# The HGRN stage of a two-block network: logarithms and scans of the two directions as two items, and the forget weights' split two slots later

## The chip, the cores and the metric

The kernel runs on one core of one Trainium2 chip. The metric is the device time of one execution in microseconds; lower is better. A core has five engines that run their own instruction lists in order and meet through semaphores: TensorE (PE, matmuls), VectorE (DVE), ScalarE (ACT), GpSimd (POOL) and SyncE (SP, which here issues DMAs).

## The reference

`first_block` (a macaron block: feed-forward, token mixing, feed-forward) is followed by `second_block` (sparse attention beside a state-space mixer, then a convolutional feed-forward); 512 positions and 256 context positions, 1024 channels. The change lies in the HGRN branch of the token mixing of the first block: eight heads of 128 channels, in two directions. Cut to what matters:

```
def _hgrn_gates(f_pre, lb):
    logf = jnp.log(lb + (1.0 - lb) * jax.nn.sigmoid(fp))
    k = (1.0 - lb) * jax.nn.sigmoid(-fp)

def _hgrn_scan(q, k, v, logf, S):   # S_t = diag(f_t) S_{t-1} + k_t v_t^T, o_t = S_t^T q_t
        b = jnp.cumsum(lf, axis=2)
        decay = jnp.exp(jnp.where(mask, b_t - b_s, -jnp.inf))
        attn = jnp.einsum('bhtd,bhtsd,bhsd->bhts', qc, decay, kc)
        o = einsum(qc * jnp.exp(b), S) + einsum(attn, vc)
        S_new = jnp.exp(b_last)[..., None] * S + einsum(kc * jnp.exp(b_last - b), vc)
```

The forget preactivations `f` (for both directions), `q`, the gate `g` and the values `v` are projections of the normalised input, in fp32.

## The kernel before

All products of this stage are three TensorE passes: each weight block and each input is split into an upper part (rounded to the matmul's 32 bit format) and a lower part (the rest), and the passes are upper by upper, upper by lower and lower by upper. ACT makes the upper part of a weight block of 128 x 2048 (`split_hi1`, L926), DVE the lower one (`split_lo1`, L935).

`hgrn_items` (L1320) writes one list `HG`, and every engine walks through this list with its own code for each kind of item. So the list sets the order on every engine at once. For each head h there are 14 slots, i = 0 to 13:

- `("fill", h+1, i)`, i = 0 to 9: the projections of the next head on PE, forget weights whf at i = 0 to 5, weights of q and gate whqg at i = 6 to 9. ACT takes them out of PSUM (L1497) into the buffers `hd`.
- `("gates", h+1)` behind slot 9: four sigmoids on ACT (L1518, L1520, with a table load), the key scale on DVE (L1590, L1594). The fill of slot 9 follows it, with two sigmoids (L1501, L1502), two DVE multiplies (L1572, L1574) and a second table load (L684).
- `("logs", h+1)`: for each direction j a logarithm on ACT (L1508) and on DVE a scan over 512 and one over 256 positions (L1581, L1583).
- `("prep", h, n)`: factors of level n of head h: four differences on POOL (L1452, L1453), an exponential on ACT (L1536), three multiplies on DVE (L1613, L1615 twice). The differences of direction j wait for its scan. prep (h+1, 0) stands in slot 11, prep (h+1, 1) in slot 13.
- `("prod", h, n)`: PE's product of these factors; `("sel", h, n)`: DVE copies its part into `at` (L1633) and so frees the product's PSUM bank.
- `("state", h, j, 2)`: a copy (L1654) and three multiply-adds (L1659) on DVE. `("v", u, i)`: a value projection on PE in slots 10 to 12 of heads 0 to 5, and its add on DVE (L1601).
- `("split", key)`: the two halves of a weight block. whf of head h+2 is first used by fill (h+2, 0), in slot 0 of head h+1.

PSUM has eight banks that go round in a ring: a bank is taken again in the order in which it was given back. In heads 0 to 5, fill (h+1, 0) of the next head's slot 0 takes the bank that sel (h, 4) frees. `both_parts` (L943) makes PE wait for DVE's lower half before the first matmul with a weight block. The buffers of upper halves are a ring of two.

In head 6 slot 10 also holds `("split", ("wgate", 0, 1024))`, and in head 7 slots 0 to 2 the first products of the next stage on the same input ("early"), for which ACT and DVE split its rows anew (L1531, L1622). Head 7 has no fills.

Of the kernel before, what the change touches and what calls it, by code (L numbers as in the profile page):

```python
# [10 lines left out]
ALU = mybir.AluOpType  # L11
ACT = mybir.ActivationFunctionType
# [325 lines left out]
def build(nc, dr, out_dram, ctx):  # L338
# [57 lines left out]
    def cst(n):  # L396
        o, c = COFF[n]
        return CSTS[:, o:o + c]

    ident, ones = cst("ident"), cst("ones")  # L400
# [10 lines left out]
    lb, olb, mx, e0, e1 = [sm(16).rearrange("p (d h) -> p d h", d=2) for _ in range(5)]  # L411
# [37 lines left out]
    def twice(name, n):  # L449
# [19 lines left out]
    HD = [{n: al("hd", w) for n, w in (("q", 512), ("gs", 512), ("b0", 768), ("b1", 768), ("k0", 768), ("k1", 768))}  # L469
          for _ in range(2)]  # L470
# [843 lines left out]
    LEAD = 2  # L1314
# [5 lines left out]
    def hgrn_items():  # L1320

        out = [("fill", 0, 0), ("split", value_key(0, 0))] + [("fill", 0, p) for p in (1, 3, 4, 6, 7, 8, 2, 5)]
        out += [("gates", 0), ("fill", 0, 9), ("split", ("whf", 1, 2048)), ("logs", 0)] + [("v", 0, i) for i in range(6)] + [("prep", 0, n) for n in range(LEAD)]
        for h in range(8):
            for i in range(14):
                n = i // 2
                out += [("state", h, j, s) for j, s in {3: [(0, 0)], 5: [(0, 1)], 6: [(1, 0)], 7: [(0, 2)], 8: [(1, 1)],
                                                        10: [(1, 2)]}.get(i, [])]
                fill = [("fill", h + 1, i)] if i < 10 and h < 7 else []
                out += fill if i < 9 else []  # L1330
                if i in (10, 11, 12) and h < 6:
                    out.append(("v", h // 2 + 1, 3 * (h % 2) + i - 10))
                if i == 1 and h < 7:
                    out.append(("split", ("whqg", h + 1, 2048)))
                if i == 6 and h < 6:
                    out.append(("split", value_key(h // 2 + 1, 3 * (h % 2))))
                out += {(6, 10): [("split", ("wgate", 0, 1024))], (6, 13): [("rows", 0), ("rows", 1)],
                        (7, 0): [("rows", 2), ("rows", 3)], (7, 1): [("split", ("wmq", 0, 2048))],
                        (7, 6): [("split", ("wmq", 1, 2048))], (7, 12): [("split", ("wmv", 0, 2048))]}.get((h, i), [])
                out += [("early", n) for n in {(7, 0): [1], (7, 2): [0], (7, 4): [2], (7, 6): [3], (7, 8): [4],  # L1340
                                               (7, 10): [5]}.get((h, i), [])]
                out += [("drain", n) for n in {(7, 6): [0], (7, 8): [1], (7, 10): [2], (7, 12): [3]}.get((h, i), [])]
                if i in (2, 3) and h:
                    out.append(("out", h - 1, i - 2))
                if i == 1:
                    out.append(("diag", h))
                if i % 2:
                    out.append(("prod", h, n))
                    if i == 13:
                        out.append(("sel", h, 6))  # L1350
                    if n + LEAD < 7:
                        out.append(("prep", h, n + LEAD))
                    elif h < 7:
                        out.append(("prep", h + 1, n + LEAD - 7))
                elif n:
                    out.append(("sel", h, n - 1))
                if i == 9 and h < 7:
                    out += [("gates", h + 1)] + fill
                    out += [("split", ("whf", h + 2, 2048))] if h < 6 else []
                    out.append(("logs", h + 1))  # L1360
        return out + [("out", 7, 0), ("out", 7, 1)]

    HG = hgrn_items()
    fP, fA, fV = sig("hg_fill_pe"), sig("hg_fill_act"), sig("hg_fill_dve")
# [110 lines left out]
    def act_hgrn(e, w):  # L1475
        for item, *a in HG:
# [25 lines left out]
                    e.activation(SB[1], z["gs"], ACT.Sigmoid).then_inc(*fA.of(h, "sg"))  # L1502
                    logs(e)
            elif item == "logs":
                h, = a
                for j in range(2):
                    b = HD[h % 2][f"b{j}"]
                    e.activation(b, b, ACT.Ln, scale=olb[:, j, h:h + 1], bias=lb[:, j, h:h + 1]).then_inc(*fA.of(h, "ln", j))  # L1508
            elif item == "gates":
                h, = a  # L1510
                z = HD[h % 2]
                w.wait_ge(*fA.at(h, "b1", "c"))
                if h >= 2:
                    w.wait_ge(*eV.at(h - 2, 6, "k", 1))
                    w.wait_ge(*stV.at(h - 2, 1, "k"))
                    w.wait_ge(*pP.at("d", h - 2))
                for j in range(2):
                    e.activation(z[f"k{j}"], z[f"b{j}"], ACT.Sigmoid, scale=-1.0).then_inc(*fA.of(h, "k", j))  # L1518
                    w.wait_ge(*fA.at(h, "k", j))
                    e.activation(z[f"b{j}"], z[f"b{j}"], ACT.Sigmoid).then_inc(*fA.of(h, "b", j))  # L1520
                w.wait_ge(*fA.at(h, "b", 1))
            elif item == "split":
                split_hi1(e, w, a[0], hg_hi)
            elif item == "v" and (a[1] == 5 or a[1] == 2 and a[0]):
                hg_hi.give((value_key(*a),), (vP, *a))
            elif item == "early" and a[0] in (0, 3, 5):
                hg_hi.give((EARLY[a[0] // 2],), (mlP, *early_name(a[0])))
            elif item == "rows":
                w.wait_ge(*rowsB.at("x"))
                for k in (2 * a[0], 2 * a[0] + 1):  # L1530
                    e.activation(x1h[:, k, :], xmf[:, k, :], ACT.Copy).then_inc(*rwA.of(k))  # L1531
            elif item == "prep":
                h, n = a
                r = EB[(7 * h + n) % 4]
                w.wait_ge(*rG.at(h, n, "k", 1))
                e.activation(r, r, ACT.Exp).then_inc(*rA.of(h, n))  # L1536
            elif item == "state":
                h, j, s = a
                d, b = DD[j], HD[h % 2][f"b{j}"]
                if s == 0:  # L1540
                    w.wait_ge(*sG.at(h, j, "c"))
                    e.activation(KS, KS, ACT.Exp).then_inc(*stA.of(h, j, "s"))
                    if h:
                        w.wait_ge(*oP.at(h - 1, "o"))
                    e.activation(d["qi"], b[:, 0:512], ACT.Exp).then_inc(*stA.of(h, j, "qi"))
                    e.activation(d["dc"], rows(b[:, 0:512], 4)[:, :, 127 if j == 0 else 0],
                                 ACT.Exp).then_inc(*stA.of(h, j, "dc"))
                elif s == 1:
                    w.wait_ge(*stP.at(h, j, "t1"))
                    e.activation(d["kn"][:, 0:512], banks("t1", h, j), ACT.Copy).then_inc(*stA.of(h, j, "k1"))  # L1550
                    w.wait_ge(*stP.at(h, j, "t2"))
                    e.activation(d["kn"][:, 512:768], banks("t2", h, j)[:, 0:256], ACT.Copy).then_inc(*stA.of(h, j, "k2"))
            elif item == "out":
                h, s = a
                if s == 0:
                    w.wait_ge(*oP.at(h, "o"))
                    w.wait_ge(*(fV.at(h + 1, "q") if h < 7 else oV.at(6, "u")))
                    e.activation(SB[0], banks("o", h), ACT.Square).then_inc(*oA.of(h, "sq"))
                else:
                    w.wait_ge(*oP.at(h, "m"))  # L1560
                    e.activation(SB[0], banks("m", h), ACT.Ln, scale=1.0 / 128, bias=eps).then_inc(*oA.of(h, "ln"))
                    w.wait_ge(*oA.at(h, "ln"))
                    e.activation(SB[0], SB[0], ACT.Exp, scale=-0.5).then_inc(*oA.of(h, "exp"))

    def dve_hgrn(e, w):
        for item, *a in HG:
# [6 lines left out]
                    w.wait_ge(*fA.at(h, "sg"))  # L1573
                    e.tensor_tensor(z["gs"], z["gs"], SB[1], ALU.mult).then_inc(*fV.of(h, "g"))  # L1574
            elif item == "logs":
                h, = a
                for j in range(2):
                    b, sgn = HD[h % 2][f"b{j}"], 1 - 2 * j
                    rm = cst("rmF") if j == 0 else cst("rmB")
                    w.wait_ge(*fA.at(h, "ln", j))  # L1580
                    e.tensor_tensor_scan(b[:, 0:512][:, ::sgn], rm[:, ::sgn], b[:, 0:512][:, ::sgn], 0.0, ALU.mult,  # L1581
                                         ALU.add).then_inc(*fV.of(h, "b", j))
                    e.tensor_tensor_scan(b[:, 512:768][:, ::sgn], ones[:, 0:256], b[:, 512:768][:, ::sgn], 0.0, ALU.mult,  # L1583
                                         ALU.add).then_inc(*fV.of(h, "c", j))
            elif item == "gates":
                h, = a
                z = HD[h % 2]
# [1831 lines left out]
```

## Time and profile before

| | |
|---|---|
| median of 3 runs | 2807.14 us (2803.46 to 2825.7) |
| span of the profiled execution | 2803.7 us |
| PE busy | 2656.1 us, 95% |
| DVE busy | 1520.1 us, 54% |
| ACT busy | 1003.3 us, 36% |
| POOL busy | 455.4 us, 16% |
| chain that ended last | PE 80%, DVE 10%, ACT 6% |

The profiled execution is one run; its span is the time between its first and last instruction, and an engine's busy share does not say what it waits for. The chain that ended last is followed back from the last instruction, each step to what released it. The HGRN stage lies between about 620 and 1110 us, with one head about each 55 us.

### The profile page before, as it was taken

How to read it: one execution, taken by the hardware profiler on the slowest of the kernel's cores; microseconds unless marked ns; L12 is line 12 of the kernel's file. 1: busy time of each engine (PE TensorE's matmuls, PEld its weight loads, DVE VectorE, ACT ScalarE, POOL GpSimd, SP SyncE). 2: the span in 40 equal slices, each digit the busy share in tenths (PEclk: the TensorE clock that was granted, in tenths of full speed). 3: DMA queues.
4: the chain of work that ended last, by engine and by line, in shares of the span. 5: the costliest groups of instructions: out<-in, count | busy, mean ns of one | idle time of the engine just before them, and what ended most of it. 6: DMA issues, size and time to landing. Idle time of an engine off the chain costs nothing.

```text
span 2803.7 us, 33123 instructions
## 1 busy us (share of the span) xinstructions
PE 2656.1 (95%) x13604; PEld 2178.6 (78%) x13604; DVE 1520.1 (54%) x2358; ACT 1003.3 (36%) x1464; POOL 455.4 (16%) x474
## 2 busy tenths in 40 slices
PE   7999999999999988999999989999798999999998
PEld 3888888879888877966888768888567655788786
DVE  4765455458777777357632465455543454543444
ACT  4212111236555553134422333223422236443343
POOL 0101000114454352000000000001011241020110
PEclk9999999999999999998999999999997699999999
DMA  7444444413211112020222233323213312222221
GB/s 296 152 187 177 169 185 177 165 45 128 75 54 68 50 72 79 31 90 1 82 99 104 86 108 126 126 106 140 108 66 108 83 53 79 105 94 100 100 85 43
DMA packets 58246, 294.59 MB, mean 105 GB/s; under 512 B 14704, under 2 KB 19952, under 8 KB 30192
## 3 DMA queue, kind: packets, MB, share of 16 engines
q1 hardware_dynamic: 56944, 282.52, 27.7%
q10 hardware_dynamic: 1152, 9.96, 0.9%
q8 instruction: 107, 1.75, 0.2%
q14 instruction: 43, 0.35, 0.0%
HBM read 271.75 MB, written 20.71 MB: 104 GB/s over the span
## 4 chain that ended last, share of the span: by engine, by line
PE 80%; DVE 10%; ACT 6%; issue 2%; POOL 1%; DMA 1%; SPq 0%; DVEq 0%; POOLq 0%; ACTq 0%
PE ps L314 78%; DVE wl L935 1%; POOL rp L2961 1%; DVE hd L1581 1%; PE ps L3110 1%; ACT x L1536 1%; ACT wh L926 0%; DMA x<-in_x 0%; DVE x L1615 0%; ACT hd L1520 0%; ACT L684 0%; DVE t L964 0%; ACT hd L1518 0%; DVE hd L1583 0%; ACT q L688 0%
## 5 line engine op out<-in xcount | busy, mean ns | idle before, releaser
L314 PE MATMUL ps<-xs,wh 128*128 128x512 f32 (+1 forms) x2816 | 786.4, 366 | 18.0 <-DVE xs L969 13.9
L314 PEld LDWEIGHTS ps<-xs,wh 128*128 128x128 f32 x2816 | 509.6, 190 | 105.4 <-issue 16.8
L314 PE MATMUL ps<-xs,wl 128*128 128x512 f32 (+1 forms) x1408 | 513.7, 365 | 0.0
L314 PE MATMUL ps<-h,wh 128*128 128x512 f32 (+1 forms) x1408 | 389.9, 363 | 7.8 <-POOL h L1168 7.8
L919 DVE TENSOR_TENSOR wl<-w,wh 128x2048 fp32r<-128x2048 f32 (+4 forms) x114 | 244.1, 2143 | 243.6 <-ACT wh L913 243.4
L913 ACT ACTIVATE wh<-w 128x2048 fp32r<-128x2048 f32 (+4 forms) x114 | 204.3, 1794 | 309.6 <-PE ps L314 272.7
L314 PEld LDWEIGHTS ps<-xs,wl 128*128 128x128 f32 x1408 | 267.8, 190 | 42.5
L314 PEld LDWEIGHTS ps<-h,wh 128*128 128x128 f32 x1408 | 252.7, 189 | 50.9 <-POOL h L1168 9.5
L314 PE MATMUL ps<-x1h,wh 128*128 128x512 f32 x584 | 242.6, 415 | 26.4 <-DVE at L1633 17.0
L314 PE MATMUL ps<-h,wl 128*128 128x512 f32 (+1 forms) x704 | 255.2, 363 | 0.0
L314 PE MATMUL ps<-x1lr,wh 128*128 128x512 f32 x584 | 236.0, 404 | 0.0
L314 PE MATMUL ps<-x1h,wl 128*128 128x512 f32 x584 | 235.2, 403 | 0.0
L1168 POOL TENSOR_TENSOR h<-t,h 128x512 fp32r<-128x512 f32 x66 | 74.6, 1134 | 851.3 <-ACT h L1069 851.3
L935 DVE TENSOR_TENSOR wl<-w,wh 128x2048 fp32r<-128x2048 f32 (+1 forms) x56 | 131.2, 2344 | 130.5 <-ACT wh L926 130.4
L1069 ACT ACTIVATE h<-t 128x512 fp32r<-128x512 f32 x66 | 37.0, 560 | 345.8 <-DVE t L1109 345.8
L314 PEld LDWEIGHTS ps<-x1h,wh 128*128 128x128 f32 x584 | 114.0, 195 | 53.5 <-issue 24.1
L926 ACT ACTIVATE wh<-w 128x2048 fp32r<-128x2048 f32 (+1 forms) x56 | 106.2, 1898 | 135.4 <-PE ps L314 118.3
L314 PEld LDWEIGHTS ps<-h,wl 128*128 128x128 f32 x704 | 132.8, 189 | 20.8
L1146 DVE SCALAR_TENSOR_TENSOR x<-ps,small,x 128x512 f32<-128x512 f32 x80 | 59.9, 749 | 149.4 <-PE ps L314 149.4
L883 DVE SCALAR_TENSOR_TENSOR w<-w,cb 128x1024 f32<-128x1024 f32 x104 | 123.9, 1221 | 29.7 <-DMA w<-in_adat 29.7
L314 PEld LDWEIGHTS ps<-x1h,wl 128*128 128x128 f32 x584 | 113.7, 195 | 27.4
L1109 DVE TENSOR_TENSOR t<-t,ps 128x512 f32<-128x512 f32 x66 | 39.5, 598 | 171.9 <-PE ps L314 159.5
(488 smaller groups left out, 4572.9 us busy)
## 6 DMA issues: line engine op xcount, KB each, us to landing
w<-in_adat SPq DMA_DIRECT2D x52, 1024.0 KB, 5.1
w<-in_f1i SPq DMA_DIRECT2D x22, 1024.0 KB, 6.5
w<-in_f2i SPq DMA_DIRECT2D x22, 1024.0 KB, 4.8
w<-in_f3i SPq DMA_DIRECT2D x22, 1024.0 KB, 4.8
s_tables<-t ACTq DMA_DIRECT2D x4, 2368.0 KB, 8.2
w<-in_ada SPq DMA_DIRECT2D x8, 1024.0 KB, 9.5
w<-in_whf SPq DMA_DIRECT2D x8, 1024.0 KB, 4.8
w<-in_whqg SPq DMA_DIRECT2D x8, 1024.0 KB, 4.8
```

The lines of the kernel that those rows point to most:

```text
L314: return e.matmul(out, l, r, start=st, stop=sp)
L883: e.scalar_tensor_tensor(out=JUNK if c + 1 < nv else wv, in0=wv, scalar=1.0, in1=v, op0=ALU.mult, op1=ALU.mult, accum_out=dst).then_inc(*m ...
L913: e.activation(hi[:, 0:key[2]], ap, ACT.Copy).then_inc(*hiA.of(key))
L919: e.tensor_tensor(lo[:, 0:key[2]], ap, hi[:, 0:key[2]].bitcast(F32), ALU.subtract).then_inc(*loV.of(key))
L926: e.activation(hi[:, 0:key[2]], ap, ACT.Copy).then_inc(*hiA.of(key))
L935: e.tensor_tensor(below(key), ap, high(key)[:, 0:key[2]].bitcast(F32), ALU.subtract).then_inc(*loV.of(key))
L1069: e.activation(hh_[:, q, o:o + T], s[:, 0:T], ACT.Copy).then_inc(*hidA.of(F.name, j, x))
L1109: e.tensor_tensor(s, s, banks(F.name, j, 1, x)[:, 0:T], ALU.mult).then_inc(*gateV.of(F.name, j, x))
L1146: e.scalar_tensor_tensor(out=dst[:, m, :], in0=banks(F.name, n, "dn", m, x)[:, 0:T], scalar=g[:, m:m + 1], in1=dst[:, m, :], op0=ALU.mult, ...
L1168: e.tensor_tensor(hl_[:, q, o:o + T], s, hh_[:, q, o:o + T].bitcast(F32), ALU.subtract).then_inc(*hidP.of(F.name, j, x))
L1536: e.activation(r, r, ACT.Exp).then_inc(*rA.of(h, n))
L1581: e.tensor_tensor_scan(b[:, 0:512][:, ::sgn], rm[:, ::sgn], b[:, 0:512][:, ::sgn], 0.0, ALU.mult, ALU.add).then_inc(*fV.of(h, "b", j))
```

## The change

The item `("logs", h)` becomes two items, `("logs", h, 0)` and `("logs", h, 1)`. The first stays behind the fill of slot 9. The second stands at the end of slot 10, behind sel (h, 4). The split of whf for head h+2 goes from slot 9, where it stood ahead of the logarithms, to the end of slot 11, behind prep (h+1, 0). For head 0, ahead of the loop, both halves of `logs` stand together as before.

```diff
-        out += [("gates", 0), ("fill", 0, 9), ("split", ("whf", 1, 2048)), ("logs", 0)] + [("v", 0, i) for i in range(6)] + [("prep", 0, n) for n in range(LEAD)]
+        out += [("gates", 0), ("fill", 0, 9), ("split", ("whf", 1, 2048)), ("logs", 0, 0), ("logs", 0, 1)] + [("v", 0, i) for i in range(6)] + [("prep", 0, n) for n in range(LEAD)]
...
                 if i == 9 and h < 7:
-                    out += [("gates", h + 1)] + fill
-                    out += [("split", ("whf", h + 2, 2048))] if h < 6 else []
-                    out.append(("logs", h + 1))
+                    out += [("gates", h + 1)] + fill + [("logs", h + 1, 0)]
+                if i == 10 and h < 7:
+                    out.append(("logs", h + 1, 1))
+                if i == 11 and h < 6:
+                    out.append(("split", ("whf", h + 2, 2048)))
...
             elif item == "logs":
-                h, = a
-                for j in range(2):
-                    b = HD[h % 2][f"b{j}"]
-                    e.activation(b, b, ACT.Ln, scale=olb[:, j, h:h + 1], bias=lb[:, j, h:h + 1]).then_inc(*fA.of(h, "ln", j))
+                h, j = a
+                b = HD[h % 2][f"b{j}"]
+                e.activation(b, b, ACT.Ln, scale=olb[:, j, h:h + 1], bias=lb[:, j, h:h + 1]).then_inc(*fA.of(h, "ln", j))
```

DVE's code for `logs` (the two scans) changes in the same way, from a loop over j to j as an argument.

DVE at the end of head 0, before (hd63 and hd64 are the logarithms of directions 0 and 1 of head 1, wl0 and wh52 the lower and upper halves of whf of head 2, at75 takes the selections, ps1 to ps7 are banks):

```order
L935 TENSOR_TENSOR wl0<-w1,wh52 128x2048
L1581 SCALAR_TENSOR_TENSOR hd63<-cst3,hd63 128x512
L1583 SCALAR_TENSOR_TENSOR hd63<-cst3,hd63 128x256
L1581 SCALAR_TENSOR_TENSOR hd64<-cst3,hd64 128x512
L1583 SCALAR_TENSOR_TENSOR hd64<-cst3,hd64 128x256
L1654 COPY dd73<-ps2 128x128
L1659 SCALAR_TENSOR_TENSOR dd73<-dd73,dd74,ps2 128x128 x3
L1601 TENSOR_TENSOR v50<-ps4,xc6 128x256
L1633 COPY_PREDICATED at75<-m8,ps1 128x512
L1601 TENSOR_TENSOR v50<-ps3,xc6 128x256
L1613 TENSOR_TENSOR x4<-x4,hd61 128x512
L1615 TENSOR_TENSOR x4<-x4,hd65 128x4x64
```

The same place in the changed kernel, from the second scan of direction 0 on:

```order
L1583 SCALAR_TENSOR_TENSOR hd63<-cst3,hd63 128x256
L1654 COPY dd73<-ps2 128x128
L1659 SCALAR_TENSOR_TENSOR dd73<-dd73,dd74,ps2 128x128 x3
L1601 TENSOR_TENSOR v50<-ps4,xc6 128x256
L1633 COPY_PREDICATED at75<-m8,ps1 128x512
L1581 SCALAR_TENSOR_TENSOR hd64<-cst3,hd64 128x512
L1583 SCALAR_TENSOR_TENSOR hd64<-cst3,hd64 128x256
L1601 TENSOR_TENSOR v50<-ps3,xc6 128x256
L1613 TENSOR_TENSOR x4<-x4,hd61 128x512
L1615 TENSOR_TENSOR x4<-x4,hd65 128x4x64
L1615 TENSOR_TENSOR x4<-x4,hd66 128x4x64
L935 TENSOR_TENSOR wl0<-w1,wh52 128x2048
```

The selection out of ps1 has moved ahead of hd64's scans, and the split wl0 from the front to behind the multiplies of prep.

ACT at the same place, before (the logarithms work in place on hd63 and hd64, L1536 is prep's exponential):

```order
L684 ACT_TABLE_LOAD
L926 ACTIVATE wh52<-w1 128x2048
L1508 ACTIVATE hd63<-hd63,small5 128x768
L1508 ACTIVATE hd64<-hd64,small5 128x768
L1536 ACTIVATE x4<-x4 128x1024 x2
```

And ACT in the changed kernel, whose lines are numbered one higher there:

```order
L684 ACT_TABLE_LOAD
L1509 ACTIVATE hd63<-hd63,small5 128x768
L1509 ACTIVATE hd64<-hd64,small5 128x768
L1537 ACTIVATE x4<-x4 128x1024
L926 ACTIVATE wh52<-w1 128x2048
L1537 ACTIVATE x4<-x4 128x1024
```

The logarithms stand right behind the table load, still as a pair; the upper split stands between prep's two exponentials.

DVE at the end of head 6, where wgate is split (128x1024), in the changed kernel; before, hd64's two scans (L1581, L1583) stood right ahead of the copy L1654:

```order
L1583 SCALAR_TENSOR_TENSOR hd63<-cst3,hd63 128x256
L1654 COPY dd73<-ps1 128x128
L1659 SCALAR_TENSOR_TENSOR dd73<-dd73,dd74,ps1 128x128 x3
L935 TENSOR_TENSOR wl0<-w1,wh51 128x1024
L1633 COPY_PREDICATED at75<-m8,ps7 128x512
L1581 SCALAR_TENSOR_TENSOR hd64<-cst3,hd64 128x512
L1583 SCALAR_TENSOR_TENSOR hd64<-cst3,hd64 128x256
L1613 TENSOR_TENSOR x4<-x4,hd61 128x512
L1615 TENSOR_TENSOR x4<-x4,hd65 128x4x64
```

The wgate split and the selection now come ahead of hd64's scans, and the multiplies right behind them. The order on PE and POOL is the same in both kernels.

## Rows read from the trace of the kernel before

**Rows 1.** Waits of PE, 600 to 1110: us in total, times, longest.

```profile
PE ps L314 <- DVE at L1633: 17.0, 6, 2.8
PE ps L314 <- DVE wl L935: 8.4, 1, 8.4
...
PE ps L314 <- DVE x1lr L1622: 3.4, 1, 3.4
```

**Rows 2.** Timeline of PE where head 2 starts: start, us, instruction, idle time before.

```profile
771.35 0.47 PE L314 MATMUL ps<-x1h,wh 128*128 128x512 f32 x1 [2.82 <-DVE at L1633]
...
774.16 0.63 PE L314 MATMUL ps<-x1h,wl 128*128 128x512 f32 x1
774.58 0.63 PE L314 MATMUL ps<-x1h,wh 128*128 128x512 f32 x1
...
776.48 0.40 PE L314 MATMUL ps<-x1h,wh 128*128 128x512 f32 x1
776.71 0.40 PE L314 MATMUL ps<-x1lr,wh 128*128 128x512 f32 x1
```

**Rows 3.** Timeline of DVE at the end of head 1.

```profile
762.38 2.29 DVE L935 TENSOR_TENSOR wl<-w,wh 128x2048 fp32r<-128x2048 f32 x1 [2.46 <-ACT wh L926]
764.59 1.22 DVE L1581 TENSOR_TENSOR_SCAN hd<-cst,hd 128x512 f32<-128x512 f32 x1
...
766.31 1.58 DVE L1581 TENSOR_TENSOR_SCAN hd<-cst,hd 128x512 f32<-128x512 f32 x1
...
768.76 0.26 DVE L1654 COPY dd<-ps 128x128 f32<-128x128 f32 x1
...
770.49 0.72 DVE L1633 COPY_PREDICATED at<-m,ps 128x512 f32<-128x512 uint8 x1
771.10 0.41 DVE L1601 TENSOR_TENSOR v<-ps,xc 128x256 f32<-128x256 f32 x1
771.43 0.69 DVE L1613 TENSOR_TENSOR x<-x,hd 128x512 f32<-128x512 f32 x1
...
773.58 0.41 DVE L1601 TENSOR_TENSOR v<-ps,xc 128x256 f32<-128x256 f32 x1
```

**Rows 4.** Timeline of ACT at the end of head 1.

```profile
760.43 1.92 ACT L926 ACTIVATE wh<-w 128x2048 fp32r<-128x2048 f32 x1
762.25 1.94 ACT L1508 ACTIVATE hd<-hd,small 128x768 f32<-128x768 f32 x2
769.86 1.06 ACT L1536 ACTIVATE x<-x 128x1024 f32<-128x1024 f32 x1 [5.67 <-POOL x L1453]
```

**Rows 5.** Busy us of engines, granted clock, DMA about two head starts and after a stall.

```profile
711.00:723.00 12.00, 9.17 (x33) 7.29 (x32) 10.66 (x18) 2.11 (x2) 12.00 (x16) 0.72 0.26 87
768.00:780.00 12.00, 9.18 (x43) 7.55 (x43) 10.14 (x17) 3.37 (x4) 12.00 (x17) 0.86 0.26 89
...
1045.60:1054.00 8.40, 8.40 (x50) 7.76 (x51) 8.40 (x10) 7.28 (x10) 8.40 (x10) 0.82 0.04 18
```

**Rows 6.** Timeline of POOL at the end of head 1.

```profile
765.95 0.85 POOL L1452 TENSOR_TENSOR x<-hd 128x256 f32<-128x256 f32 x1 [19.97 <-DVE hd L1581]
...
768.26 1.00 POOL L1452 TENSOR_TENSOR x<-hd 128x256 f32<-128x256 f32 x1
769.22 0.61 POOL L1453 TENSOR_TENSOR x<-hd 128x256 f32<-128x256 f32 x1
```

**Rows 7.** Timelines of DVE and POOL, the split of head 2's slot 1.

```profile
781.27 2.76 DVE L935 TENSOR_TENSOR wl<-w,wh 128x2048 fp32r<-128x2048 f32 x1 [2.85 <-ACT wh L926]
...
781.84 2.78 POOL L1452 TENSOR_TENSOR x<-hd 128x256 f32<-128x256 f32 x1
```

**Rows 8.** Timelines of DVE and PE where head 7 starts.

```profile
1044.15 1.34 DVE L935 TENSOR_TENSOR wl<-w,wh 128x1024 fp32r<-128x1024 f32 x1
1046.03 1.07 DVE L1613 TENSOR_TENSOR x<-x,hd 128x512 f32<-128x512 f32 x1
...
1045.54 0.58 PE L314 MATMUL ps<-c1h,wh 128*128 128x256 f32 x1 [8.40 <-DVE wl L935]
```

More of the change, by code:

```diff
@@ L1575, in dve_hgrn @@
             elif item == "logs":
[L1576 to L1584, printed above, removed]
+                h, j = a
+                b, sgn = HD[h % 2][f"b{j}"], 1 - 2 * j
+                rm = cst("rmF") if j == 0 else cst("rmB")
+                w.wait_ge(*fA.at(h, "ln", j))
+                e.tensor_tensor_scan(b[:, 0:512][:, ::sgn], rm[:, ::sgn], b[:, 0:512][:, ::sgn], 0.0, ALU.mult,
+                                     ALU.add).then_inc(*fV.of(h, "b", j))
+                e.tensor_tensor_scan(b[:, 512:768][:, ::sgn], ones[:, 0:256], b[:, 512:768][:, ::sgn], 0.0, ALU.mult,
+                                     ALU.add).then_inc(*fV.of(h, "c", j))
             elif item == "gates":
```

## Prediction

> **What bounds the kernel now.** I began with the whole-program page: TensorE (PE) is busy 95% of the span and the chain that ended last lies on it for 80%. So a change in the HGRN stage is worth what it does to PE's idle time and to PE's clock, and nothing else. The next view was the list of waits of PE in that stretch [rows 1]. Three of its lines touch the change: six waits for the selection L1633 (17.0 us together, 2.83 each), one of 8.4 us for a weights' split L935, and one of 3.4 us for the rows' lower parts L1622. The six stand at one place in each of heads 0 to 5: the first matmul of the next head's first projection, `("fill", h+1, 0)`, for example at 771.35 [rows 2]. Within the six heads the list has no other wait of PE, so nothing behind the start can take up a delay of it.
>
> Why it waits there: the matmul needs a PSUM bank that the selection `("sel", h, 4)` frees, and the split whf h+1, i.e. both halves of the weights it multiplies with. Today the split ends at 764.67 and is never late; the selection ends at 771.21 and is [rows 3]. On VectorE (DVE) the split, four scans, four state instructions and a value add stand ahead of that selection without a break, and the first of them waits for ScalarE (ACT), whose run through sigmoids, table load, split and logarithms ends at 764.19 [rows 4].
>
> The stall has a second price. After each the matmuls go at 0.43 us start to start (774.16 to 774.58) where later ones go at 0.23 (776.48 to 776.71) [rows 2]: the granted clock is at the lower of its two levels, 1.2 instead of 2.4 GHz. Of the 12 us stretches about the six starts, four have a mean granted clock of 0.86 and two have 0.72 [rows 5], so the low clock lasts 12 x 0.14 x 2 = 3.4 us or 6.7 us, and a low microsecond loses 0.46 (1 - 0.23/0.43): 1.5 or 3.1, 2.1 on the mean.
>
> **The change, part by part.** No instruction is added or removed; two moves in each of seven heads and a third, of the whf split, in six.
>
> *(a) The split whf leaves the front of the logarithms.* ACT's first logarithm starts at 760.43, where the upper split starts now; half the pair's 1.94 makes the first scan start at 761.45 instead of 764.59 [rows 3, 4]. Then two scans of direction 0 (764.59 to 766.31, 1.72), state and value add (768.76 to 770.49, 1.73), selection 4 (0.61 to the next start). It ends near 765.6, which is 2.9 before PE asks for the bank (771.35 - 2.82 = 768.53). The old wait is gone: taken alone, 6 x (2.83 + 2.1) = 30 us, at most.
>
> *(b) The second direction's scans go behind the selection.* They start at 765.5. The 512-wide one takes 1.22 with GpSimd (POOL) idle and 1.58 beside it; POOL's differences for direction 0 will be done by then, so 1.22, to 766.7 [rows 3, 6].
>
> *(c) The split whf goes behind the next head's first factor, `("prep", h+1, 0)`.* This is the step that decides. The same matmul at 768.53 needs the split just as it needs the bank. DVE runs its list in order, and the factor's multiplies L1613/L1615 stand ahead of the split. They need ACT's exponential, this needs POOL's last difference, and this needs the second scan. Step by step: scan done 766.7; POOL starts 0.14 later (765.95 against 764.59 + 1.22); its last two differences take 1.57 (768.26 to 769.83); the exponential starts 0.03 later and takes 1.06, to 769.5 [rows 4, 6]. The multiplies take 2.15 (771.43 to 773.58), to 771.7 [rows 3]. ACT's upper split (1.92) runs meanwhile, 769.5 to 771.4, and is just hidden. Then DVE's lower split.
>
> Its length: 2.29 today, with POOL idle until 765.95; the one at 781.27, beside a busy POOL, takes 2.76 [rows 3, 6, 7]. In the new place POOL is busy all of 768 to 780 [rows 5], so I take 2.7, and the nearer bound of 2.2 for the low end. The Trainium skill, GPSIMD Engine Reference, Key points, has the reason: GpSimd shares its SBUF interfaces with VectorE and they contend when a VectorE instruction reads two SBUF inputs, as this one does. By that rule the split costs 2.7, without it 2.2, 3 us over six heads; the rows agree with the rule.
>
> So the split ends at 774.4 and PE starts there, not at 771.35: **+3.05 us per head**. With everything at its shortest (multiplies uncontended, split right behind ACT's 771.4, 2.2) it is 773.6, +2.3. With the direction 0 differences of POOL and the scans in each other's way (0.36 more on the scan, 0.4 on POOL) it is +3.8. The stall grows from 2.83 to 5.9. Six heads: **+18.3** (14 to 23).
>
> What queues behind the late split on DVE: a value add and selections 5 and 6. PE wants their banks only some 9 us into the next head (a later fill and output), so they cost nothing. The whf DMA and the order of both buffer rings do not move: SyncE (SP) and POOL pass over both items. The pair of logarithms on ACT stays back to back.
>
> *(d) Head 6, where the split behind is wgate.* There is no whf split, but the second scans move behind the wgate split and selection. That split starts 2.45 earlier (766.31 to 768.76 is the length of a scan pair), 1041.7 instead of 1044.15, and PE's 8.4 us wait shrinks to 5.9 [rows 3, 8]. It is given back: the second scan starts at 1043.6 (1041.7 + 1.3 + 0.61), so its POOL differences and exponential end at 1043.6 + 1.22 + 0.14 + 1.57 + 0.03 + 1.06 = 1047.6, and L1613 starts then instead of at 1046.03 [rows 8]. DVE runs without a gap from there to the L1622 for which PE waits 3.4 us [rows 1]; all of it is 1.6 late. **+1.6**, whatever the earlier gain.
>
> *(e) The clock.* The longer stall (5.9) can leave the low stretch at 3.4 us or move it to 6.7. After the 8.4 us stall the clock was low for 8.4 x 0.18 x 2 = 3.0 us, no longer than after the short ones [rows 5], so I add only 0.3 per head, **+2** (bounds -3, all six short, and +6, all six long).
>
> Sum: 18.3 + 1.6 + 2 = 22 us on the profiled execution, whose span of 2803.7 lies 3.4 below the median of 2807.14. On the median: **2829 us**, +0.8%.
>
> **The rivals.**
> *R1, the stall costs more:* in all six heads the clock stays low for 6.7 us (+6 instead of +2) and the DVE/POOL overlap takes the +3.8 bound (+23): 23 + 1.6 + 6 = 31, 2838. For it: POOL is busy throughout. Against: a shifted start makes the direction 0 differences run while DVE reads from PSUM.
> *R2, about even:* the split follows quickly and the delay is absorbed, 2.3 per head at the low clock bound, or part of it taken up before the next head's gates: 0 to +11, 2807 to 2818. Against: PE has no gap in between, so each head's gates start as much later as its fills.
> *R3, faster:* the matmul does not find the split late. That needs the split's end before 771.3, 3 us ahead of my sum; it decides there, head by head. If it holds, at best the stall and its clock loss go: 30 us less, 2777. What speaks for it: selection 4 really is 5.6 us earlier. Against: the split stands behind three engines' hand-offs, each with its row.
> *R4, the change does nothing:* excluded, the instruction lists differ in all seven heads.
>
> **How the numbers follow.** Forecast (2819 to 2835): 0.62. R1: 0.19. R2: 0.14. R3: 0.05. Leaving out R3, the lower third of R2 and the far end of R1 gives a range of 2811 to 2842. About 1% (28 us) is what a measurement of this kernel can tell from no change: its three runs lie 22 us apart. Slower by over 1% means beyond 2835: R1 and an edge of the forecast, 0.22. Faster by over 1% is R3 with nearly its full gain, 0.03. Within 1%: 0.75.
>
> **What would show it.** In the profile after: (1) selection L1633 four ends before PE's last product of the head; if not, (a) is wrong. (2) PE's waits list names L935 six times at 5.5 to 6.2 us, and L1633 no more; if it names L1633 or L1615, the chain is other than I think. (3) L935 of whf starts near 11.3 us behind the table load's end (760.42 here) and takes 2.7; 2.3 would mean POOL is not in the way. (4) ACT's first exponential starts some 8 us behind that load instead of 9.4. (5) In head 7 the wgate wait is near 5.9 and the L1622 wait near 7. (6) The granted clock of the six 12 us stretches stays between 0.72 and 0.86. The prediction falls if L935 of whf ends before the head's last product does, or if fills of a later head wait for the split longer than 7 us.

## The result and the profile after

The changed kernel takes 2832.73 us (median of 15 runs, 2819.47 to 2845.45), the kernel before 2807.14 (median of 15, 2795.38 to 2825.7). The ratio is 1.0083, with a 95% interval of 1.0061 to 1.0104: slower by 0.8%. The profiled execution has a span of 2819.9 us, 16.2 more than the 2803.7 of before.

PE's list of waits, 600 to 1140 us of the profile after, answers to [rows 1]:

```profile
PE ps L314 <- DVE wl L935: 43.8, 7, 6.3
PE ps L314 <- DVE x1lr L1622: 4.4, 3, 3.4
...
PE ps L314 <- DVE x L1615: 0.8, 1, 0.8
```

The selection L1633 is gone from the list. In its place stands the whf split L935: seven waits, six of 6.33 us at the starts of heads 1 to 6 and one of 5.83 for wgate. The place is the same as in [rows 2]; here are the first matmuls of head 1 and head 6 in both kernels, PE's timeline, before first:

```profile
714.89 0.77 PE L314 MATMUL ps<-x1h,wh 128*128 128x512 f32 x1 [2.83 <-DVE at L1633]
...
993.25 0.47 PE L314 MATMUL ps<-x1h,wh 128*128 128x512 f32 x1 [2.83 <-DVE at L1633]
```

```profile
720.27 0.80 PE L314 MATMUL ps<-x1h,wh 128*128 128x512 f32 x1 [6.33 <-DVE wl L935]
...
1016.53 0.80 PE L314 MATMUL ps<-x1h,wh 128*128 128x512 f32 x1 [6.33 <-DVE wl L935]
```

From the one to the other are 278.4 us before and 296.3 after: 17.9 more over five heads, and 5 x 3.50 of it is the longer wait (6.33 against 2.83).

The timeline of DVE at the end of head 1 answers to [rows 3]. ACT's table load, at which this chain begins, ends at 764.53 here, 4.11 later than the 760.42 of before; the two loads, before first:

```profile
759.14 1.28 ACT L684 ACT_TABLE_LOAD   x1
...
763.25 1.28 ACT L684 ACT_TABLE_LOAD   x1
```

And DVE behind it:

```profile
765.61 1.23 DVE L1581 TENSOR_TENSOR_SCAN hd<-cst,hd 128x512 f32<-128x512 f32 x1 [1.57 <-ACT hd L1509]
...
769.06 0.73 DVE L1633 COPY_PREDICATED at<-m,ps 128x512 f32<-128x512 uint8 x1
769.69 1.21 DVE L1581 TENSOR_TENSOR_SCAN hd<-cst,hd 128x512 f32<-128x512 f32 x1
...
773.65 1.10 DVE L1613 TENSOR_TENSOR x<-x,hd 128x512 f32<-128x512 f32 x1 [1.86 <-ACT x L1537]
...
776.22 2.70 DVE L935 TENSOR_TENSOR wl<-w,wh 128x2048 fp32r<-128x2048 f32 x1
```

Selection 4 (769.06) starts 5.5 us sooner than before, counted from the table load (770.49 - 760.42 = 10.07 there, 769.06 - 764.53 = 4.53 here). Then DVE stands idle for 1.86 us ahead of L1613, at 773.65, and the split starts behind the multiplies at 776.22. ACT's timeline of the same place, to [rows 4], and POOL's, to [rows 6], show whom L1613 waited for:

```profile
764.55 1.95 ACT L1509 ACTIVATE hd<-hd,small 128x768 f32<-128x768 f32 x2
772.50 1.06 ACT L1537 ACTIVATE x<-x 128x1024 f32<-128x1024 f32 x1 [6.00 <-POOL x L1455]
773.46 1.89 ACT L926 ACTIVATE wh<-w 128x2048 fp32r<-128x2048 f32 x1
```

```profile
770.97 0.92 POOL L1454 TENSOR_TENSOR x<-hd 128x256 f32<-128x256 f32 x1 [2.57 <-DVE hd L1581]
771.86 0.60 POOL L1455 TENSOR_TENSOR x<-hd 128x256 f32<-128x256 f32 x1
```

POOL's last two differences start 0.07 us behind the end of the second scan (769.69 + 1.21 = 770.90), the exponential right behind them, the multiplies behind that. ACT's upper split (773.46 + 1.89) ends before the multiplies do and delays nothing.

The stretches of 12 us about the starts of heads 1 and 2, to [rows 5] (stretch and length; busy us of PE, of its weight loads, of DVE, ACT and POOL; granted clock; DMA), and last the 3.9 us just before PE's first matmul of head 2 at 778.97:

```profile
716.90:728.90 12.00, 8.63 (x37) 7.23 (x38) 7.40 (x8) 1.94 (x3) 9.18 (x10) 0.72 0.02 10
775.60:787.60 12.00, 8.63 (x26) 6.87 (x27) 7.40 (x8) 0.72 (x1) 9.17 (x10) 0.60 0.04 13
```

```profile
775.00:778.90 3.90, 0.00 (x0) 0.00 (x0) 3.90 (x4) 1.32 (x2) 3.90 (x4) 0.50 0.23 97
```

Their mean granted clock is 0.72 and 0.60; over the six starts it is 0.60 or 0.61 twice and 0.72 or 0.73 four times. Part of that low clock now falls into the wait itself, as the last row shows, where it costs nothing. Behind the matmuls that end the waits it lasts, read in steps of 1 us, about 27.1 us over the six starts, against 25.5 before.

Counted from the start of the HGRN stage (behind PE's one wait of 3.9 us for L1309) to a short wait with no releaser shortly before its end, both present in every profile of this study, the stage takes 483.2 us before and 507.2 after: **24.0 more**, which is the 0.8% of the timed runs. That the two profiled spans differ by 16.2 only is down to the rest of the program, which is the same in both kernels and was 7.8 us shorter in this one execution. Between runs of one kernel the time moves by 26 us with the clock that PE is granted (0.961 at 2819.47 us, 0.951 at 2845.45), so below the whole time is compared by its ratio and the mechanism by stretches of the stage.

### The profile page after: what moved, and what is told of

The parts are those of the page before. It is cut to its first block, busy times and chain, and to the rows that moved or that the text cites. A ratio compares the mean times of both kernels' runs of the same rounds, so it can differ in the third digit from the quotient of the medians.

```text
span 2819.9 us, 33123 instructions
## 1 busy us (share of the span) xinstructions
PE 2649.5 (94%) x13604; PEld 2174.9 (77%) x13604; DVE 1516.8 (54%) x2358; ACT 1003.4 (36%) x1464; POOL 460.6 (16%) x474
## 4 chain that ended last, share of the span: by engine, by line
PE 79%; DVE 10%; ACT 6%; issue 2%; POOL 1%; DMA 1%; SPq 1%; DVEq 0%; POOLq 0%; ACTq 0%
PE ps L314 78%; DVE wl L935 1%; ACT x L1537 1%; POOL rp L2961 1%; DVE x L1615 1%; DVE hd L1581 1%; DVE x L1613 0%; DMA x<-in_x 0%; PE ps L3110 0%; ACT hd L1521 0%; ACT L684 0%; ACT hd L1519 0%; ACT q L688 0%; DVE gr L2074 0%; DVE at L1633 0%
## 5 line engine op out<-in xcount | busy, mean ns | idle before, releaser
L314 PE MATMUL ps<-xs,wh 128*128 128x512 f32 (+1 forms) x2816 | 787.1, 366 | 17.6 <-DVE xs L969 13.6
L314 PEld LDWEIGHTS ps<-xs,wh 128*128 128x128 f32 x2816 | 510.1, 191 | 104.8 <-issue 16.2
L314 PEld LDWEIGHTS ps<-h,wh 128*128 128x128 f32 x1408 | 252.8, 189 | 51.3 <-POOL h L1168 10.0
L935 DVE TENSOR_TENSOR wl<-w,wh 128x2048 fp32r<-128x2048 f32 (+1 forms) x56 | 132.1, 2361 | 134.1 <-ACT wh L926 134.0
L1454 POOL TENSOR_TENSOR x<-hd 128x256 f32<-128x256 f32 x112 | 105.7, 944 | 184.5 <-DVE hd L1581 160.8
```

The source lines that it names most:

```text
L314: return e.matmul(out, l, r, start=st, stop=sp)
L935: e.tensor_tensor(below(key), ap, high(key)[:, 0:key[2]].bitcast(F32), ALU.subtract).then_inc(*loV.of(key))
L1454: e.tensor_tensor(rq[:, :, qh, :], b4[:, :, qh, :], mid, ALU.subtract).then_inc(*rG.of(h, n, "q", j))
```

## The experiments

"Head 1 to head 6" is the stretch between the two matmuls shown above. "Stage" is the one just described. "Ratio" is against the kernel before on the same chip.

| kernel | wait at each of six starts | head 1 to head 6 | stage | ratio (95%) |
|---|---|---|---|---|
| before | 2.83 (L1633) | 278.4 | 483.2 | 1 |
| changed | 6.33 (L935) | 296.3 | 507.2 | 1.0083 (1.0061 to 1.0104) |
| e1_scans_only | 0.37 (L1633) | 256.3 | 458.6 | 0.9927 (0.9888 to 0.9966) |
| e2_split_only | 4.73 (L935) | 289.5 | 497.3 | 1.0028 (0.9999 to 1.0056) |
| e3_split_behind_sel | none | 252.8 | 455.6 | 0.9885 (0.9822 to 0.9948) |
| e4_split_before_prep | 1.46 (L935) | 261.3 | 466.5 | 0.9949 (0.9918 to 0.9979) |
| e6_head7_together | 6.33 (L935) | 296.1 | 505.3 | one execution |
| e7, split behind sel, scans together | 2.17 (L935) | 272.8 | 476.9 | 1.0000 (0.9980 to 1.0020) |
| e8_best | none | 252.8 | 453.1 | 0.9901 (0.9885 to 0.9918) |

Two notes on reading it. Where an experiment's kernel.py is shorter by two lines (e2 and e7), the same instructions have line numbers lower by two: L1579, L1581, L1611, L1613 and L1631 there are L1581, L1583, L1613, L1615 and L1633 here. And the stages of e3 and e4 hold 1.6 us that lie away from what their edits touch: from the wait of 1.95 us for L1627 to the end of the stage there are 19.2 us in these two and 17.6 in the other seven, because only in these two the clock fell there; what made it fall is not shown.

**The scans alone.** The split goes back ahead of the logarithms; nothing else of the change is undone.

```diff
-                    out += [("gates", h + 1)] + fill + [("logs", h + 1, 0)]
+                    out += [("gates", h + 1)] + fill
+                    out += [("split", ("whf", h + 2, 2048))] if h < 6 else []
+                    out.append(("logs", h + 1, 0))
...
-                if i == 11 and h < 6:
-                    out.append(("split", ("whf", h + 2, 2048)))
```

> The two halves of the logarithms stay apart as in the changed kernel, but the whf split stands ahead of them again, as before. The theory (the late split is what costs, the earlier selection alone is a gain): by the kernel before's own times the split ends at 764.6, selection 4 at about 768.8, PE asks at 768.53, so PE's wait at each of the six starts falls from 2.83 to about 0.4 us, with perhaps 0.5 more for prep's product, and the low clock behind it mostly goes: about 4 us per start less than before, +1.6 at head 7, in all 22 us less than before (ratio 0.992). From the start of head 1 to the start of head 6: about 258 us (278.4 before, 296.3 in the changed kernel). The rival (the scans' new place, with POOL beside them, is what costs): PE still waits 4 us or more at each start and the time stays above before's, ratio 1.00 to 1.01.

PE's waits, 640 to 1140, and the busy table of a start's 12 us:

```profile
PE ps L314 <- DVE at L1633: 2.2, 6, 0.4
```

```profile
761.00:773.00 12.00, 11.63 (x77) 10.43 (x76) 9.95 (x16) 5.46 (x5) 9.44 (x14) 1.00 0.25 89
```

The wait fell to 0.37 (0.4 expected), the granted clock is 1.00, the stretch 256.3 (258 expected), and the kernel is faster than before. So the half of the change that moves the second scans is a gain of 24.6 us in the stage, and the rival, which put the cost there, falls.

**The split alone.**

```diff
-                    out += [("gates", h + 1)] + fill + [("logs", h + 1, 0)]
-                if i == 10 and h < 7:
-                    out.append(("logs", h + 1, 1))
+                    out += [("gates", h + 1)] + fill + [("logs", h + 1, 0), ("logs", h + 1, 1)]
```

> The whf split alone moves to the end of slot 11, behind prep; both directions' logarithms and scans stay together behind the fill of slot 9. The theory: the split is late by itself. The scans start at 761.45, POOL's differences end at about 766.7, the exponential at 767.8, prep's multiplies run behind selection 4 until about 771, the split takes 2.7: PE waits for L935 at the six starts, about 5.1 us each (2.83 before, 6.33 in the changed kernel), head 7 is as before; in all 14 us above before (ratio 1.005). Head 1 to head 6: about 290 us. The rival (only both moves together make it slow, the split being late because the second scan is): PE waits under 3 us and the time is within 5 us of before's.

PE's waits, and DVE's timeline at the end of head 1:

```profile
PE ps L314 <- DVE wl L935: 36.8, 7, 8.4
```

```profile
769.26 0.73 DVE L1631 COPY_PREDICATED at<-m,ps 128x512 f32<-128x512 uint8 x1
769.88 0.41 DVE L1599 TENSOR_TENSOR v<-ps,xc 128x256 f32<-128x256 f32 x1
770.21 0.69 DVE L1611 TENSOR_TENSOR x<-x,hd 128x512 f32<-128x512 f32 x1
770.83 1.62 DVE L1613 TENSOR_TENSOR x<-x,hd 128x256 f32<-128x256 f32 x2
772.37 2.70 DVE L935 TENSOR_TENSOR wl<-w,wh 128x2048 fp32r<-128x2048 f32 x1
```

The six waits of 4.73 (5.1 expected) and the one of 8.40 for wgate make the 36.8. Here the multiplies do not wait for ACT, they start right behind the selection and the value add, and the split is still 1.9 us later than the bank was before: its place is late by itself, and the stage is 14.1 us longer than before (14 expected). The timed runs alone do not settle it, as the ratio's interval just reaches 1. Together with the first experiment this splits the 3.50 us of the change. The place behind the multiplies costs 1.90, and the second scans, moved behind the selection, hold the multiplies up and add 1.60 to it.

**The split ahead of the factor.** One line of the changed kernel, the split at the end of slot 10, behind the second scans.

```diff
-                if i == 11 and h < 6:
+                if i == 10 and h < 6:
                     out.append(("split", ("whf", h + 2, 2048)))
```

> As the changed kernel, but the whf split stands behind the second scans and ahead of prep, so that it no longer waits for POOL and the exponential. The theory: DVE is free for it at 767.3 in the times of the kernel before, it takes 2.2 to 2.7, so PE's wait for L935 is about 1.3 us instead of 6.33. Against before: 1.5 less per start in waits and 0 to 2 in low clock, +1.6 at head 7: 7 to 19 us less than before, 13 taken (ratio 0.995). Head 1 to head 6: 265 us. The rival (the split's own length beside POOL is what counts, not the queue ahead of it): the wait stays above 4 us.

DVE's timeline at the end of head 1 and the busy table of that start:

```profile
763.81 1.20 DVE L1581 TENSOR_TENSOR_SCAN hd<-cst,hd 128x512 f32<-128x512 f32 x1
764.93 0.66 DVE L1583 TENSOR_TENSOR_SCAN hd<-cst,hd 128x256 f32<-128x256 f32 x1
765.52 2.64 DVE L935 TENSOR_TENSOR wl<-w,wh 128x2048 fp32r<-128x2048 f32 x1
```

```profile
766.00:778.00 12.00, 10.55 (x67) 9.34 (x67) 10.56 (x12) 5.56 (x5) 12.00 (x15) 1.00 0.24 89
```

With POOL busy all 12 us, and the split as long as in the changed kernel (2.64 against 2.70), the wait is 1.46 instead of 6.33. So 4.9 of the 6.3 us are the queue ahead of the split (POOL, exponential, multiplies), not the split; the rival falls. The stage is 16.7 us shorter than before against 13 expected, because the clock does not fall at all behind the six waits of 1.46 (without the 1.6 of the later stretch it would be 18.3).

**The split right behind the selection.**

```diff
+                if i == 10 and h < 6:
+                    out.append(("split", ("whf", h + 2, 2048)))
                 if i == 10 and h < 7:
                     out.append(("logs", h + 1, 1))
-                if i == 11 and h < 6:
-                    out.append(("split", ("whf", h + 2, 2048)))
```

> Logarithms apart as in the changed kernel; the whf split stands right behind selection 4 and ahead of the second direction's scans. The theory: selection 4 ends at 765.6, the split at 767.9, both ahead of PE's 768.53; the second scan ends at 769.1, POOL at 770.7, the exponential at 771.8, prep's multiplies at 774.4, just ahead of the 774.9 at which PE wants their product. So PE has no wait at the six starts and keeps the high clock: 6 x (2.83 + 2.1) less, 1.6 more at head 7: 28 us less than before (ratio 0.990). Head 1 to head 6: 254 us. The rival (the clock falls at these places whatever the wait, or prep's product becomes the wait): a gain of 17 us or less, with L1615 in PE's list of waits.

DVE's timeline at the end of head 1, and the busy table of the 257 us from head 1 on:

```profile
759.67 0.72 DVE L1633 COPY_PREDICATED at<-m,ps 128x512 f32<-128x512 uint8 x1
760.30 2.27 DVE L935 TENSOR_TENSOR wl<-w,wh 128x2048 fp32r<-128x2048 f32 x1
762.49 1.21 DVE L1581 TENSOR_TENSOR_SCAN hd<-cst,hd 128x512 f32<-128x512 f32 x1
...
766.47 1.11 DVE L1613 TENSOR_TENSOR x<-x,hd 128x512 f32<-128x512 f32 x1 [1.87 <-ACT x L1537]
```

```profile
711.00:968.00 257.00, 257.00 (x1717) 233.16 (x1717) 223.78 (x294) 155.24 (x196) 141.47 (x163) 1.00 0.18 63
```

The split takes 2.27, as POOL stands idle meanwhile, and ends at 762.57, 0.4 ahead of PE's first matmul of head 2 (763.01 in this execution). PE is busy for 257.00 of 257.00 us at a granted clock of 1.00. Prep's multiplies end at 769.06 and do not become the wait. Theory and measurement agree (252.8 against 254 from head 1 to head 6; 27.6 us less in the stage against 28).

**The same with the scans together**, to see what moving the second scans is worth.

```diff
-                    out += [("gates", h + 1)] + fill + [("logs", h + 1, 0)]
+                    out += [("gates", h + 1)] + fill + [("logs", h + 1, 0), ("logs", h + 1, 1)]
                 if i == 10 and h < 6:
                     out.append(("split", ("whf", h + 2, 2048)))
-                if i == 10 and h < 7:
-                    out.append(("logs", h + 1, 1))
```

> As e3_split_behind_sel, but both directions' scans stay together ahead of the selection: the whf split behind selection 4, and nothing else changed against before. The theory (moving the second scans behind the selection is worth their own length on DVE): the scans run from 761.45 to 765.65, selection 4 to 768.1, the split beside POOL to 770.7: PE waits for L935 about 2.1 us at each of the six starts, where e3 had none. Head 1 to head 6: 270 us (e3: 252), time 3 to 8 us under before's (ratio 0.998). The rival (the split's place alone makes the gain of e3, the scans' place is worth nothing): no wait, and the time of e3, ratio 0.99.

```profile
761.26 1.58 DVE L1579 TENSOR_TENSOR_SCAN hd<-cst,hd 128x512 f32<-128x512 f32 x1
762.76 1.03 DVE L1581 TENSOR_TENSOR_SCAN hd<-cst,hd 128x256 f32<-128x256 f32 x1
...
765.45 0.73 DVE L1631 COPY_PREDICATED at<-m,ps 128x512 f32<-128x512 uint8 x1
766.07 2.62 DVE L935 TENSOR_TENSOR wl<-w,wh 128x2048 fp32r<-128x2048 f32 x1
```

```profile
767.00:779.00 12.00, 10.26 (x51) 8.80 (x52) 8.67 (x12) 3.91 (x4) 11.13 (x13) 0.86 0.20 80
```

The second scan of 512 takes 1.58 and that of 256 takes 1.03 with POOL at work on direction 0, and the split 2.62 instead of 2.27. The wait of 2.17 (2.1 expected) is enough to lower the clock to 0.86, so the stretch is 20.0 us longer than in e3: 5 x 2.17 of waits, and most of the rest low clock (3.4 us a head, of which 0.46 is lost: 7.8 over five). The stage is 6.3 us shorter than before; the timed runs (ratio 1.0000, 0.9980 to 1.0020) do not show that 0.2%, which lies at the edge of their interval.

**Head 7.** The changed kernel, with the two halves of the logarithms together in head 6 alone.

```diff
-                    out += [("gates", h + 1)] + fill + [("logs", h + 1, 0)]
-                if i == 10 and h < 7:
+                    out += [("gates", h + 1)] + fill + [("logs", h + 1, 0)] + ([("logs", 7, 1)] if h == 6 else [])
+                if i == 10 and h < 6:
                     out.append(("logs", h + 1, 1))
```

> The changed kernel, with the two halves of the logarithms together again at the end of head 6 alone. The theory (step d: the scans behind the wgate split cost 1.6 us although PE's wait for that split is shorter): PE's wait for L935 of wgate is back at 8.4 us (5.83 in the changed kernel), the waits for L1615 and the short ones for L1622 are gone, and from the first matmul of head 6 to the one behind the wait of 3.4 us for L1622 there are 64.9 us as before, not the changed kernel's 66.7. The rival (DVE has slack there and the later scans cost nothing): the stretch stays at 66.7. The whole time, one execution, cannot show it.

PE's waits where head 7 starts, in the changed kernel, in the kernel before (the second wait; the first is in [rows 8]) and in this one:

```profile
1066.59 0.58 PE L314 MATMUL ps<-c1h,wh 128*128 128x256 f32 x1 [5.83 <-DVE wl L935]
...
1073.74 1.16 PE L314 MATMUL ps<-x 128*128 128x128 f32 x8 [0.82 <-DVE x L1615]
...
1083.19 0.79 PE L314 MATMUL ps<-x1h,wh 128*128 128x512 f32 x1 [3.38 <-DVE x1lr L1622]
```

```profile
1058.16 0.50 PE L314 MATMUL ps<-x1h,wh 128*128 128x512 f32 x1 [3.38 <-DVE x1lr L1622]
```

```profile
1069.58 0.58 PE L314 MATMUL ps<-c1h,wh 128*128 128x256 f32 x1 [8.40 <-DVE wl L935]
...
1082.20 0.54 PE L314 MATMUL ps<-x1h,wh 128*128 128x512 f32 x1 [2.22 <-DVE x1lr L1622]
```

In the changed kernel PE gets wgate after 5.83 us, then waits in front of L1615 and L1622, and is through at 1083.19: 22.4 us after it ran out of work (1066.59 - 5.83). In this one it waits 8.40 and is through 21.0 us after, as in the kernel before (1037.14 to 1058.16). So the scans' place costs 1.4 there, though the first wait is shorter. DVE shows the way: L1613, the first of prep's multiplies, starts 10.3 us behind the moment at which PE ran out of work in the changed kernel (1071.04) and 8.9 behind it in this one (1070.08) and before (1046.03). The expected stretch of 64.9 from head 6 on came out at 65.3, since a low clock at head 6's start is in it; measured from where PE ran out, the 1.4 is clean. The wait of 3.4 for L1622 also became 2.2, for the same low clock: PE came to it later, and it ended when it ended.

**The best of it.** e3 for heads 0 to 5, the logarithms together in head 6 as just shown, and the wgate split two slots earlier.

```diff
-                out += {(6, 10): [("split", ("wgate", 0, 1024))], (6, 13): [("rows", 0), ("rows", 1)],
+                out += {(6, 8): [("split", ("wgate", 0, 1024))], (6, 13): [("rows", 0), ("rows", 1)],
```

> e3_split_behind_sel for heads 0 to 5; at the end of head 6 the logarithms stay together and the wgate split moves from slot 10 to slot 8, where DVE and ACT wait for others. The theory: nothing of wgate is left on the way to head 7's prep, whose multiplies start at 1044.9 in the times of before (1046.03 before, 1047.6 in e3), so the rows' split L1622, for which PE waits, ends 1.2 us sooner than before and 2.8 sooner than in e3. PE's wait for L935 goes, and most of its length comes back as a wait for L1615 or L1622, since the same DVE work bounds this place. 33 us less than before, ratio 0.988 (e3: 0.9885). The rival (the wait for the wgate split itself was what cost PE there): PE is 5 us or more earlier at the place behind the wait for L1622 than in e3, ratio 0.985.

```profile
1019.73 2.08 PE L314 MATMUL ps<-x 128*128 128x128 f32 x8 [7.77 <-DVE x L1615]
...
1029.17 0.50 PE L314 MATMUL ps<-x1h,wh 128*128 128x512 f32 x1 [3.37 <-DVE x1lr L1622]
```

```profile
999.65 1.07 ACT L926 ACTIVATE wh<-w 128x1024 fp32r<-128x1024 f32 x1
...
1001.69 1.28 ACT L1519 ACT_TABLE_LOAD   x1
```

The wait for wgate is gone and most of it came back, 7.8 us in front of L1615, so the rival (5 us or more) falls. But the theory's own number did not come out either. From the first matmul of head 6 to the one behind the wait for L1622 there are 63.3 us (965.92 to 1029.17) and in e3 64.8 (965.22 to 1029.98): 1.5 sooner, not 2.8. That is the 1.4 of the logarithms together, so the wgate split's new place, which was to add 1.2, gave next to nothing. ACT had no free time there: its upper split of 1.07 us now runs ahead of the table load of the gates, which starts 35.8 us behind the first matmul of head 6 instead of 34.8 (1000.04 in e3), and everything behind it on ACT and DVE is as much later. The stage is 2.4 us shorter than in e3, near the expected 2.8 by accident: 1.5 from here, 0.6 lost to a longer low clock behind the L1622 wait, and the 1.6 of the later stretch. Ratio 0.9901 (0.9885 to 0.9918), 2777.57 us against 2806.79 on the same chip. It beats the kernel before. That it also beats e3 (ratio 0.9885 with a wider interval, on another chip) the timed runs do not show, and of the stage's 2.4 us only 0.8 is left without the later stretch.

## Why the prediction was right

The forecast was 2829 us for a measured 2832.73, and its mechanism is the one that the profile shows.

- *(a) right.* Scan 1 starts 1.08 us behind the table load (1.03 forecast) and selection 4 starts 4.5 behind it; the wait for L1633 is gone. e1 has 24.6 us for the scans' half of it, and e3, with nothing put in the way, 27.6 of the 30 that it was priced at.
- *(b) right.* The second 512-wide scan takes 1.21 (1.22), with POOL idle.
- *(c) right in kind, 0.45 too short.* 3.50 per start, not 3.05; six starts are 21.0, not 18.3. The term of the sum that was too small is the multiplies: 2.15 was taken, from a place where the first of them ran in 0.69. They take 2.57 here (773.65 to 776.22), since L1613 itself takes 1.10. POOL works on the next level's differences at this moment in both kernels; what differs is where in them L1613 starts. In the changed kernel it starts 0.06 to 0.08 us behind the start of a difference at all six starts and takes 1.10, in the kernel before 0.48 to 0.50 behind and takes 0.68 or 0.69:

```profile
770.94 0.62 POOL L1452 TENSOR_TENSOR x<-hd 128x256 f32<-128x256 f32 x1
```

```profile
773.59 0.62 POOL L1454 TENSOR_TENSOR x<-hd 128x256 f32<-128x256 f32 x1
```

(Before, beside L1613 at 771.43 [rows 3], and in the changed kernel, beside L1613 at 773.65.) The other terms hold: POOL's pair 1.49 (1.57), exponential 1.06, split 2.70 (2.7). Between the bounds of the split the row beside a busy POOL was the one to take, and the reading that the Trainium skill (GPSIMD Engine Reference, Key points) gives for it, contention with a VectorE instruction of two SBUF inputs, agrees with 2.70 and 2.62 beside POOL and 2.27 without.
- *(d) right.* 1.4 for 1.6. That the shorter wait is given back through prep is shown by e6, with L1613 1.4 later.
- *(e) right in the sum, not in its detail, and so in part by luck.* What is left of the stage's 24.0 after 21.0 and 1.4 is 1.6, for 2 forecast. I had put all of it at the six starts. There it is 0.7 (0.4 over the five heads measured and 0.3 in head 6), which is what the low clock behind them gives, (27.1 - 25.5) x 0.46. The other 0.8 arises behind the 3.4 us wait for L1622 in head 7, where the clock is low for 9.02 x 0.32 x 2 = 5.8 us, for 8.18 x 0.21 x 2 = 3.4 before (before first):

```profile
1058.16:1066.34 8.18, 7.47 (x37) 5.96 (x37) 7.83 (x9) 0.65 (x2) 2.57 (x3) 0.79 0.29 89
```

```profile
1083.19:1092.21 9.02, 8.33 (x36) 6.98 (x37) 7.83 (x9) 0.65 (x2) 2.57 (x3) 0.68 0.26 89
```

Against the forecast of 22 the stage's 24.0 is 2.7 more from (c), 0.2 less from (d) and 0.4 less from (e).

The rivals: R1 (2838) asked for +3.8 per start. The 3.50 are more than half way there, but not by R1's route: the second scan took 1.21 and not 0.36 more, and POOL's pair 1.49; it was the multiplies that grew. R2 did not happen, the whole wait passes to the end of the stage. (Its upper end was also added up wrongly: 6 x 2.3 + 1.6 - 3 is 12.4, not 11; nothing hangs on it.) R3, the faster outcome, needed the split before 771.3 in the times of before; its end was at 774.8. It is what e3 gives when the split is put where R3 needed it, and the 30 us forecast for it were 27.6 in the stage, or 29.2 without the later stretch's 1.6.

Of the signs named ahead, (1), (3) and (4) came in, and (2) in kind, at 6.33 and so outside 5.5 to 6.2. Of (5) the wgate wait was 5.83 for 5.9, but the waits for L1622 and L1615 together took 5.2, not 7 (the longest 3.4, as before): PE worked at the low clock and came later. (6) was wrong: two of the six stretches fell below 0.72, to 0.60. I had counted only the low clock behind the wait, not the part inside it.

## What to carry to other kernels

A matmul may wait for two things, and a profile names only the later one. Before a piece of work is moved away from the front to make the named one earlier, look up what else the same instruction waits for, and put the moved piece where it is still ahead of that instruction. An instruction that waits for two other engines is a bad thing to put in front of work that the bottleneck needs: behind the selection the split cost nothing, behind prep 6.3 us a head.

## What the runs showed of the hardware

I had not expected the clock to tell short waits apart so sharply at one place. At the head starts of these kernels, PE's waits of 0.37 and 1.46 us left the granted clock at 1.00 at all six starts. Waits of 2.17 lowered it at all six (mean 0.86 of 12 us, i.e. 1.2 instead of 2.4 GHz for 3.4 us). The waits of 2.83 gave 0.86 four times and 0.72 twice, those of 4.73 gave 0.72 six times, those of 6.33 gave 0.72 or 0.73 four times and about 0.60 twice. So a wait brought from 2.17 to 1.46 gives back three times the difference: e7 and e4 differ by 0.71 per wait and by 2.3 us per head (272.8 and 261.3 over five).

The length of the wait alone does not decide it. Behind the stage every profile has a wait of 2.13 to 2.17 us for DVE's L1895: the clock stayed at 1.00 in four of the nine (before, e2, e6, e7) and fell in five. The wait of 1.95 to 1.97 for L1627 lowered it in two of nine (e3, e4). The 7 us about the L1895 wait, before and e1:

```profile
1128.00:1135.00 7.00, 4.87 (x42) 4.67 (x41) 6.78 (x12) 3.78 (x4) 0.00 (x0) 1.00 0.01 2
```

```profile
1103.00:1110.00 7.00, 4.87 (x29) 4.67 (x28) 6.79 (x13) 3.76 (x4) 0.00 (x0) 0.76 0.00 0
```

What separates the two is not shown. And how long an instruction of DVE takes beside POOL can hang on a few tenths of a microsecond: in the kernels before and changed the same multiply (L1613, first of a head) took 0.69 when it started 0.5 us behind the start of a POOL difference and 1.10 when it started 0.07 behind (six of six each).
